# First attention with one combined VectorE operation and late division, two adaLN steps moved, and another order of ScalarE in the latent heads

## The reference

```python
# first block: attention that mixes three dilations (window, dilation):
DILATION_PATTERNS = ((128, 1), (512, 4), (2048, 16))   # 8 heads of 64
o = sum_d(wts_d * o_d) / sum_d(wts_d)   # wts_d = l_d * exp(m_d - max m)
# beside it: spatial gating u * (W_s LayerNorm(gelu(v)) + b), in chunks of 128
# adaLN: parameters of both later layers, from c and c_ctx only
m = silu(cond) @ w_ada + b_ada          # 1024 x 6144, for each of two layers
# latent attention of the last layer, 16 heads, 512 queries, 768 keys
s = einsum(q, k) * 96 ** -0.5; p = softmax(s); o = p @ v
```

## Time and profile before

| | us |
|---|---|
| median of 3 runs | 2501.7 (2501.55 to 2505.22) |
| profiled execution, and its span | 2504.9, 2503.1 |
| TensorE, VectorE, ScalarE busy | 2371.1, 1167.8, 752.2 |
| first attention | about 187 to 247 |
| experts of the first block | about 340 to 640 |
| latent heads | about 1797 to 2069 |

### The profile page before, as it was taken

The page is one execution under the profiler, slowest core; times in us unless marked ns, Lnnn a source line. Parts: engine busy times, 40 slices in busy tenths (PEclk is TensorE's granted clock), DMA queues, the critical chain, the costliest instruction groups (busy, mean ns, idle before and its releaser), DMA issues.

```text
span 2503.1 us, 29569 instructions
## 1 busy us (share of the span) xinstructions
PE 2371.1 (95%) x12236; PEld 1711.7 (68%) x12236; DVE 1167.8 (47%) x1912; ACT 752.2 (30%) x1303; POOL 224.8 (9%) x207
## 2 busy tenths in 40 slices
PE   8998999999898998899999999999888889999998
PEld 5673463333445978548888888877777767788886
DVE  2247342211564767543443343444676563544444
ACT  2235012111223345324112112123555562322222
POOL 0000011111104015100000000000202041000000
PEclk9999999999999999999999999999999999999999
DMA  9937659997410211312122112212010012223321
GB/s 350 372 130 269 247 178 391 376 379 293 164 23 31 68 51 52 135 34 82 53 68 68 61 41 84 68 34 61 30 51 5 18 68 74 86 86 101 98 86 69
DMA packets 172837, 308.80 MB, mean 123 GB/s; under 512 B 18459, under 2 KB 75155, under 8 KB 172576
## 3 DMA queue, kind: packets, MB, share of 16 engines
q1 hardware_dynamic: 159600, 278.40, 31.8%
q0 software_dynamic: 12368, 26.35, 3.0%
q10 hardware_dynamic: 736, 2.15, 0.2%
HBM read 355.05 MB, written 18.93 MB: 149 GB/s over the span
## 4 chain that ended last, share of the span: by engine, by line
PE 60%; DVE 8%; ACT 4%; issue 1%; DMA 0%; POOL 0%; DVEq 0%; ACTq 0%
PE PS L140 38%; PE PS L2593 11%; PE PS L2531 2%; PE PS L152 2%; PE PS L3180 2%; DVE X L110 1%; PE PS L2537 1%; DVE Rr L110 1%; PE PS L3101 1%; DVE H L110 1%; ACT X L130 1%; PE PS L2469 1%; DVE MIX L110 1%; DVE H L118 1%; DVE sm L121 1%
## 5 line engine op out<-in xcount | busy, mean ns | idle before, releaser
L140 PE MATMUL PS<-at,wH 128*128 128x512 f32 (+1 forms) x2144 | 564.6, 352 | 2.8 <-DVE at L110 2.8
L140 PEld LDWEIGHTS PS<-at,wH 128*128 128x128 f32 x2144 | 379.4, 190 | 57.7 <-DVE at L110 2.3
L140 PE MATMUL PS<-at,rest 128*128 128x512 f32 (+1 forms) x1072 | 377.0, 352 | 0.0
L2593 PE MATMUL PS<-wH,ac 128*128 128x512 f32 x880 | 277.8, 393 | 3.3 <-DVE hn L110 3.3
L110 DVE TENSOR_TENSOR rest<-ring,wH 128x2048 fp32r<-128x2048 f32 x66 | 150.4, 2291 | 212.6 <-ACT wH L133 212.0
L140 PEld LDWEIGHTS PS<-at,rest 128*128 128x128 f32 x1072 | 203.4, 190 | 27.1
L133 ACT CAST wH<-ring 128x2048 fp32r<-128x2048 f32 x66 | 124.6, 1906 | 264.5 <-PE PS L2593 199.8
L2593 PEld LDWEIGHTS PS<-wH,ac 128*128 128x128 f32 x880 | 165.2, 188 | 43.1 <-DVE hn L110 8.4
L2593 PE MATMUL PS<-rest,ac 128*128 128x512 f32 x440 | 171.4, 390 | 0.0
L140 PE MATMUL PS<-ring,AT 128*128 128x512 f32 x320 | 140.0, 593 | 1.4 <-ACT AT L133 0.8
L110 DVE TENSOR_TENSOR hn<-PS,gate 128x512 f32<-128x512 f32 x120 | 83.0, 692 | 104.4 <-PE PS L2593 99.4
(11 more groups left out here) (392 smaller groups left out, 4128.3 us busy)
## 6 DMA issues: line engine op xcount, KB each, us to landing
R<-in_w_gate_up_dram SPq DMA_DIRECT2D x32, 1024.0 KB
ring<-in_w_down_dram SPq DMA_DIRECT2D x32, 1024.0 KB, 14.1
ring<-in_w_gate_up_dram SPq DMA_DIRECT2D x32, 1024.0 KB
ring<-in_w_ffn_gate_dram SPq DMA_DIRECT2D x22, 1024.0 KB, 5.4
ring<-in_w_ffn_up_dram SPq DMA_DIRECT2D x22, 1024.0 KB, 5.4
ring<-in_w_ffn_down_dram SPq DMA_DIRECT2D x22, 1024.0 KB, 5.0
ring<-in_w_ada_dram SPq DMA_DIRECT2D x16, 1024.0 KB, 7.4
HIw<-in_w_gate_up_dram SPq DMA_DIRECT2D x16, 1024.0 KB
```

What stands on the lines that cost most here:

```text
L140: ins = self.e.matmul(out, l, r, start=k == 0, stop=k == len(pairs) - 1)
L2593: ins = p.e.matmul(bk(4 + n_dn % 3), a_, b_, start=start and i == 0, stop=stop and i == len(terms) - 1)
```

## The change

- The mask table is multiplied by 8. VectorE's two operations on a unit become one `tensor_tensor_reduce`: (score + 8 mask) x (-0.125), with the running minimum as second result; ScalarE's exponential takes scale -1 and that minimum as bias.
- The rows are no longer divided before they are turned; turns wait for the exponential alone. For each head pair VectorE takes 8 reciprocals at once, TensorE spreads them over 64 rows for both heads (eight products with the identity, into the bank whose turn it is, signal `linv`), VectorE copies them out, and multiplies them into o on its way from bank 5 to `mT`. ScalarE no longer copies o.
- adaLN steps 16 and 17 move from the attention into the projections: 16 behind the half product (9, 1), 17 in place of the wait for `ada_add` and of `keep_busy` before `spatial(3)`. The other six run at n = 6, 10, 14, 18, 22, 26.
- In the latent heads ScalarE exponentiates unit n before it copies the turned blocks of unit n - 2, where unit n - 2 is the first of its head.
- In the list of signal names the entries that these need are changed.

```diff
-    lnc = np.array([-1e30, 0.0, np.log(2.0), np.log(3.0)], np.float32)[c]
+    lnc = 8.0 * np.array([-1e30, 0.0, np.log(2.0), np.log(3.0)], np.float32)[c]
...
                 if n == 9 and t:
+                    if t == 1:
+                        ada_pe(p, 16)
                     spatial(t - 1)
 
         p.wait_ge(S("act1"), 15)
         scores1(p, 0)
-        p.wait_ge(S("ada_add"), 1)
-        keep_busy(p, 5, 9)
+        ada_pe(p, 17)
         spatial(3)
 
     def proj1_act(a):
@@ -804,7 +805,19 @@
...
-    ADA_AT = [n for n in range(35) if n % 8 in (4, 6)]
+    ADA_AT = [6, 10, 14, 18, 22, 26]
+    ml1 = lambda n: (sm[:, 2 * (n % 16):2 * (n % 16) + 1], sm[:, 2 * (n % 16) + 1:2 * (n % 16) + 2])
+    l8 = [sm[:, 16 * j:16 * j + 16].rearrange("p (n c) -> p n c", c=2)[:, :, 1] for j in range(2)]
+    inv8 = [sm[:, 32 + 8 * j:40 + 8 * j] for j in range(2)]
+    linv1 = AT[:, 4096:4608]
+    TURNS1 = [x for hp in range(4) for x in [("turn", 8 * hp + i) for i in range(8)] + [("inverse", hp)]]
+
+    def turned_bank(p, what):
+        i = TURNS1.index(what)
+        if i > 1:
+            kind, m = TURNS1[i - 2]
+            p.wait_ge(S("prob_T_copy" if kind == "turn" else "linv_copy"), m + 1)
+        return PTB[i % 2]
 
     def attn1_pe(p):
         p.wait_ge(S("act1"), 16)
@@ -812,7 +825,7 @@
         p.wait_ge(S("gated"), 4)
         p.wait_ge(S("v_copy"), 4)
         p.wait_ge(S("ada_add"), 1)
-        c = 16
+        c = 18
         for n in range(35):
 
             if n < 30 and n % 2 == 0:
@@ -830,56 +843,60 @@
             if 2 <= n < 34:
                 m = n - 2
                 nk, x = units1[m][1] + 1, xb[m % 4]
-                p.wait_ge(S("prob"), m + 1)
-                p.wait_ge(S("prob_T_copy"), m - 1)
-                p.turns([(bk(PTB[m % 2], 128, 128 * b), x[:, 128 * b:128 * b + 128]) for b in range(nk)], ident, S("prob_T"))
+                p.wait_ge(S("exp1"), m + 1)
+                b0 = turned_bank(p, ("turn", m))
+                p.turns([(bk(b0, 128, 128 * b), x[:, 128 * b:128 * b + 128]) for b in range(nk)], ident, S("prob_T"))
+                if m % 8 == 7:
+                    hp = m // 8
+                    p.wait_ge(S("inverse1"), hp + 1)
+                    b0 = turned_bank(p, ("inverse", hp))
+                    p.each([(PS[64 * e:64 * e + 64, 512 * b0 + 128 * t:512 * b0 + 128 * t + 128],
+                             inv8[hp % 2][:, 2 * t + e:2 * t + e + 1].to_broadcast([P, 64]), ident) for t in range(4) for e in range(2)], S("linv"))
             if n in ADA_AT:
                 ada_pe(p, c)
                 c += 1
 
     def attn1_dve(v):
-        c = 16
-        for n in range(35):
+        c = 18
+        for n in range(36):
             if n < 32:
                 h, t = units1[n]
                 w = 128 * t + 128
-                x, (m, l) = xb[n % 4], ml(n)
+                x, (m, l) = xb[n % 4], ml1(n)
                 v.wait_ge(S("score"), n + 1)
                 v.wait_ge(S("prob_T"), n - 3)
                 v.settle()
-                v.stt(x[:, 0:w], bk(SCORE[n % 4], w), 0.125, lnc[:, t, 0:w], ALU.mult, ALU.add, inc=S("masked"))
+                v.up(v.e.tensor_tensor_reduce(x[:, 0:w], bk(SCORE[n % 4], w), lnc[:, t, 0:w], -0.125, 3e38, ALU.add, ALU.min, m), S("masked"))
+            hp = n // 8 - 1
+            if hp >= 0 and n % 8 == 0:
+                v.wait_ge(S("exp1"), n)
+                v.recip(inv8[hp % 2], l8[hp % 2], inc=S("inverse1"))
+            if hp >= 0 and n % 8 == 2:
+                v.wait_ge(S("linv"), hp + 1)
+                v.copy(linv1, bk(PTB[TURNS1.index(("inverse", hp)) % 2]), inc=S("linv_copy"))
+            if hp >= 0 and n % 8 == 3:
+                v.wait_ge(S("o"), hp + 1)
                 v.settle()
-                v.red(m, x[:, 0:w], ALU.max, neg=True, inc=S("top"))
-            if 1 <= n <= 32:
-                w = 128 * units1[n - 1][1] + 128
-                x, (m, l) = xb[(n - 1) % 4][:, 0:w], ml(n - 1)
-                v.wait_ge(S("exp1"), n)
-                v.recip(l, l)
-                v.settle()
-                v.ts(x, x, l, None, ALU.mult, inc=S("prob"))
+                v.tt(mT[:, hp, :], bk(5), linv1, ALU.mult, inc=S("o_copy"))
             if n in ADA_AT:
                 ada_dve(v, c)
                 c += 1
 
     def attn1_act(a):
         a.wait_ge(S("gated"), 4)
-        c = 16
+        c = 18
         for n in range(35):
             if n < 32:
                 w = 128 * units1[n][1] + 128
-                x, (m, l) = xb[n % 4], ml(n)
-                a.wait_ge(S("top"), n + 1)
-                a.fn(x[:, 0:w], x[:, 0:w], ACT.Exp, inc=S("exp1"), bias=m, accum_out=l)
-            if n >= 3 and units1[n - 3][1] == 3 and units1[n - 3][0] % 2:
-                hp = units1[n - 3][0] // 2
-                a.wait_ge(S("o"), hp + 1)
-                a.cast(mT[:, hp, :], bk(5), inc=S("o_copy"))
+                x, (m, l) = xb[n % 4], ml1(n)
+                a.wait_ge(S("masked"), n + 1)
+                a.fn(x[:, 0:w], x[:, 0:w], ACT.Exp, inc=S("exp1"), bias=m, scale=-1.0, accum_out=l)
             if 2 <= n < 34:
                 m = n - 2
                 h, t = units1[m]
                 a.wait_ge(S("prob_T"), m + 1)
                 a.wait_ge(S("o"), h // 2)
-                a.cast(probT[h % 2][:, 0:t + 1, 128 * t:128 * t + 128], bk(PTB[m % 2], 128 * t + 128).rearrange("p (b q) -> p b q", b=t + 1),
+                a.cast(probT[h % 2][:, 0:t + 1, 128 * t:128 * t + 128], bk(PTB[TURNS1.index(("turn", m)) % 2], 128 * t + 128).rearrange("p (b q) -> p b q", b=t + 1),
                        inc=S("prob_T_copy"))
             if n in ADA_AT:
...
+        def turned(n):
+            t = units[n - 2][1]
+            a.wait_ge(S("p2_T"), 2 * (n - 2) + 1)
+            a.wait_ge(S("o2"), units[n - 2][0])
+            a.cast(pTm[:, 0:4, 128 * t:128 * t + 128], bk(4).rearrange("p (b q) -> p b q", b=4), inc=S("pT_act"))
+
         for n in range(67):
-            if 2 <= n < 66:
-                t = units[n - 2][1]
-                a.wait_ge(S("p2_T"), 2 * (n - 2) + 1)
-                a.wait_ge(S("o2"), units[n - 2][0])
-                a.cast(pTm[:, 0:4, 128 * t:128 * t + 128], bk(4).rearrange("p (b q) -> p b q", b=4), inc=S("pT_act"))
+            if 2 <= n < 66 and units[n - 2][1]:
+                turned(n)
             if n < 64:
                 x, (m, l) = pb[n % 3], ml(n)
                 b = 2 * (n % 2)
                 a.wait_ge(S("top2"), n + 1)
                 a.wait_ge(S("p2_T"), 2 * (n - 2))
                 a.fn(x, PS[:, 512 * b:512 * b + 768], ACT.Exp, inc=S("exp2"), bias=m, accum_out=l)
+            if 2 <= n < 66 and units[n - 2][1] == 0:
+                turned(n)
             if n >= 3 and units[n - 3][1] == 3:
                 h = units[n - 3][0]
```

More of the change, by code:

```diff
@@ L65 @@
     conv_w_T=("cond_T", 1), norm_w_T=("conv_w_T", 1), cq_a=("dt_raw", 2), kpe=("logit_m", 4), rows_T=("x_T", 8), proj6=("proj1", 40),
-    exp2=("exp1", 32), o2_copy=("o_copy", 4), pT_act=("prob_T_copy", 32),
+    exp2=("exp1", 32), pT_act=("prob_T_copy", 32),
     a_high=("x_high", 8), a_high0=("a_high", 8), a_high1=("a_high0", 6),
@@ L72 @@
     xb_copy=("h1_T_copy", 8), cq_copy=("z_copy", 12), cqb_copy=("cq_copy", 4), ck_copy=("g_silu", 12), kp_copy=("conv_silu", 8),
-    k_high=("conv_raw", 16), scaled=("cond", 1),
-    a_low=("x_low", 8), a_low0=("a_low", 8), a_low1=("a_low0", 6), q_low=("v_copy", 4), roped6=("roped1", 8), q_rope=("roped6", 8),
-    top2=("top", 32), prob2=("prob", 32), mixer_s=("mixer_r", 6), state_s=("state_r", 10),
+    k_high=("conv_raw", 16), scaled=("cond", 1), o2_copy=("scaled", 4),
+    a_low=("x_low", 8), a_low0=("a_low", 8), a_low1=("a_low0", 6), inverse1=("v_copy", 4), q_low=("inverse1", 4), linv_copy=("roped1", 8), roped6=("linv_copy", 4), q_rope=("roped6", 8),
+    mixer_s=("mixer_r", 6), state_s=("state_r", 10),
     gated_r=("gated", 4), y_sum_s=("gated_r", 6), z_gated=("y_sum_s", 6), v_mid=("combined", 4), gated_out0=("z_gated", 6),
@@ L78 @@
     ac_low0=("rowsD", 24), ac_low1=("ac_low0", 11), down_mul0=("y_copy0", 24), down_mul1=("down_mul0", 72),
-    down_add1=("down_add0", 72), ssd_norm=("vs_norm", 4), cq_norm=("ssd_norm", 6), ck_norm=("cq_norm", 4), k_low=("hid_T_copy", 24),
+    down_add1=("down_add0", 72), ssd_norm=("vs_norm", 4), cq_norm=("ssd_norm", 6), ck_norm=("cq_norm", 4), prob2=("ck_norm", 6), k_low=("hid_T_copy", 24),
     k_pe_low=("mixer_s", 6), cq_low=("inter_used_s", 10), ck_low=("state_s", 10), pe_low=("dt_mask", 6), wq_low=("q_decayed", 6),
```

2 lines of the change are left out of this document (1 added, 1 removed).

## The result

The changed kernel takes 2491.1 us (median of 5 runs, 2488.1 to 2491.8); beside it the kernel before took 2501.8 (2501.6 to 2505.2). The ratio is 0.9949, with a 95% interval of 0.9935 to 0.9962. The forecast was 2491.4. By the ratio the gain is 12.8 us (9.5 to 16.3) where the forecast had 10.3, so that the two medians lie 0.3 us apart is chance.

The account below looks back on a forecast made before the run. TensorE's list was taken to bound the attention, a ScalarE link the latent heads. Gains of 2.4 + 2.4 less 1.5 lost gave 3.3; with 7.0 from the heads, 10.3 off 2501.7: 2491.4 us, range 2484 to 2499.

Parts of the forecast that it names:

- the front: End of projections plus first attention: together 3.3 us earlier, bounds -2 and 8.5.
- Step 1, adaLN steps: End of projections: two adaLN steps move there and the fourth spatial product starts later; 1.5 us lost, bounds 0 and 3.3.
- Step 2, attention: First attention: VectorE's unit becomes one combined operation; 2.4 us won in the first head pair, 2.4 in the others together.
- TensorE's list: First attention: TensorE's own work, 12.2 us a head pair plus 1.0 of new products, limits what relieving VectorE can win.
- Second and third head pair: First attention: 13.2 us each against 13.59 and 13.48, so 0.4 and 0.3 us won.
- Fourth: First attention, last head pair: 11.0 us against 12.71, so 1.7 us won.
- First: First attention, first head pair: products with v at 202.0 instead of 204.4, 2.4 us won, bounds 0 and 4.5.
- Front in full: After the attention: an early gain is carried through in full, since an earlier route lets the experts' weight stream start earlier.
- rival (a): Projections and attention give nothing, TensorE being the bound already; only the heads win: 2494.7 or 2496.7 us, chance 0.16.
- Step 3, heads: Latent heads: ScalarE's exponential before its copy fits into idle time; 7.0 us won, bounds 3 and 9.
- ten links of the chain: Latent heads, where waits pass through ScalarE's copy and exponential: eight lose 0.90 us, two gain 0.47 and 0.59; 8.3 in all.
- Rival (c): Attention: the wait for a weight piece sets the low clock, which lasts through the fourth head pair; 2517 us, chance 0.06.

Follow-up runs that it names:

- experiment 5: The changed kernel again, unaltered: 2492.1 us, ratio 0.9952 to the kernel before.
- experiment 8: Changed kernel with the combined VectorE operation taken apart into mask-and-scale and a separate minimum, late division kept: 2493.8 us, ratio 0.9963 to the kernel before.
- experiment 4: Kernel before with only adaLN steps 16 and 17 moved to the end of the projections, old attention kept: 2513.9 us, ratio 1.0037.
- experiment 11: Changed kernel with the eight products that spread the reciprocals issued twice for each head pair: 2493.4 us, ratio 0.9956 to the kernel before.
- experiment 7: Changed kernel with only adaLN step 16 moved; step 17 stays in the attention, the old fillers and wait in its place: 2489.9 us, ratio 0.9943.
- experiment 2: Changed kernel with ScalarE's old order in the latent heads: 2498.3 us, ratio 0.9979 to the kernel before.
- experiment 1: Kernel before with only ScalarE's new order in the latent heads: 2494.3 us, ratio 0.9967.
- experiment 9: Kernel before with ScalarE's new order only at the ten heads where its chain of waits went over ScalarE's copy: 2494.4 us, ratio 0.9960.
- experiment 10: Kernel before with ScalarE's new order only at five other heads (1, 3, 6, 9, 11): 2503.4 us, ratio 0.9993.
- experiment 12: Changed kernel with only adaLN step 16 moved, and 28 instead of 22 fillers at the route: 2490.0 us, ratio 0.9945 to the kernel before.

## Why the prediction was right

The total was right, and so was its order: the heads first, the front second. The terms inside it were off by more than the total: the heads won more than the sum had, the adaLN steps were never seen to win, and the agreement to 0.3 us is luck.

**Step 1, adaLN steps: the mechanism right.** Step 16 in VectorE's shadow, the half product back at full speed (2.85 us, forecast 2.72), step 17 on a DMA wait at 182.38 (forecast 182.35), the fourth spatial product 1.76 us late (forecast 1.5). The clock's fall cost 1.4 us in step 17 and 0.2 in the spatial product, where 1.1 and 0.7 were forecast. In other traces the product was later, 2.8 us in experiment 5 and 3.5 in experiment 8; the stated bound of 3.3 is too low by the forecast's own terms, which give 2.1 + 1.1 + 0.7 = 3.9, and with it the front's lower bound of -2 should have been near -3. What was missing is that the same edit without the attention's costs 9 us (experiment 4). The two parts were priced one by one and summed, and in the traces they do not sum: 1.9 us for the attention and -9.6 for the steps in the front, 1.4 to 4.5 for both.

**Step 2, attention: the sum near, its parts not.** Forecast 4.8 us between the fourth spatial product and the output stage; measured 4.45 + 1.76 = 6.2 (4.2 in experiment 5). Right were the combined operation (0.69 us; its bound of 1.38 was not needed), VectorE's 5.7 us for a head pair (5.59), the spread products (1.0; 1.02) and TensorE's list as the main bound (experiment 11). Wrong was the 0.45 us for a VectorE copy of 512 columns from PSUM, which was also the lower bound of the operation: such a copy takes 0.69, in the trace before as well; VectorE had room for it. Of the operation the Trainium skill (Vector Engine (DVE) Microarchitecture Reference, 7. Points that are easy to get wrong) says half rate for two non-bf16 SBUF sources; with one source in PSUM the trace shows 691 ns, the mask-and-scale's own duration, so the rule did not apply here, and the read of the minimum, 83 ns, is the only extra.

- Second and third head pair: forecast 13.2 each, measured 13.48. TensorE's own list was 13.2 as said (13.17 busy in 13.50); what was left out is the 0.33 us in which it waits for ScalarE's copy of the turned blocks before the spread products; where the adaLN steps stand so that it does not wait, the pair takes 13.08 (experiment 7). Nothing was won in the third and 0.1 in the second, instead of 0.7 together.
- Fourth: forecast 11.0, measured 11.32.
- First: forecast 2.4 won, measured 2.90 + 1.76 = 4.7 from a later start. This is the attention's term that was most mis-sized, and it varies: 4.7 in this trace, 2.6 in that of experiment 5 (186.71 to 204.59 is 17.9 us, against 20.51). The clock was taken to rise at 197.3 as before; it was back at 193.0 in the first trace and at 198.1 in the second. The stated bound of 4.5 "by when the clock rises" is about what came.

**Front in full: supported by experiment 2,** whose time is 5.3 us less (3.0 to 7.3) and whose heads start 4.2 us earlier. The changed kernel's own two traces have the heads 0.6 earlier and 0.6 later than before, with falls of the clock on the way. Read alone, they would have supported rival (a).

**Step 3, heads: the mechanism right but not the whole of it.** Forecast 7.0 of 8.3 us, bounds 3 to 9; the stretch is 11.2 shorter in the trace, 8.3 (5 to 11) by experiment 1's ratio. The ten links of the chain held the places that pay (experiments 9 and 10). Over the steps that they touch the gains in the changed kernel are 0.8, 0.8, 2.6, 0.7, 2.4, 0.1, 0.1, 2.6, 0.2 and 0.6 us. The three large ones hold a fall of the clock before and none after: in the one shown, 0.9 is the exponential and 1.7 the products with v at 2.81 instead of 4.50. The clock has a share in the second 0.8 too: experiment 10, which does not edit that step, won 0.66 there. With 0.7 and three times 1.7 taken off, about 5.2 us are left for the links themselves, below the 7.0, since five links gave only 0.1 to 0.6: something else was next within less than 0.9, as the forecast allowed for. The missing term is the clock: nearly 6 us of the trace that the forecast did not have in its sum.

**Rival (c)** did not happen in the changed kernel, but experiment 4 is near that mechanism: a wait for a piece, a clock low through the first head pair, another fall in the last. It was argued against with "the same kinds of work present"; experiments 4 and 8 rather point to VectorE's shorter list, which leaves TensorE no stops in the changed kernel's last head pair beyond 0.56 us.

What stays open: why the clock of one and the same program falls at the experts or in the stages behind in one execution and not in another (changed kernel and experiment 2 at 340 to 350; experiments 5, 11 and 12 after 1000). That moves single traces by 3 to 4 us, as much as the whole front. Open is also whether the moved steps win anything: their gain in the front (2.6 us in one trace, none in the other) is within that spread.

## What to carry to other kernels

Where the chain of waits passes through an engine that has idled for the same releaser and then does two things, of which one was ready long ago, put the ready one first: ten such places gave 9.4 us in the trace, at five others the edit gave none. Price a stall of TensorE that goes or comes with what the clock does behind it: here that was about half of the heads' gain in the trace. Price two edits that feed the same engine together: moving two steps off the attention's list was worth -9 us with the old VectorE and was no loss with the new one. And before a trace's difference of 3 us, a hundred us away from any edit, is explained, take the same program again.

## What the runs showed of the hardware

- A VectorE multiply-add with a minimum beside it takes 691 ns for 128x512 from PSUM and SBUF in f32, as without the minimum, and is followed by a read of 83 ns; two of them stand 0.87 us apart (194.34 and 195.21).
- A VectorE copy of 512 f32 columns of 128 rows from PSUM took 692 ns here, no less than a product with a second operand (691).
- The clock fell at stops of TensorE of 2.9 to 3.2 us, in the stop or within 0.4 us of its end. It also fell at shorter ones: in one of 1.6 us (the kernel before, at 187.0), and at the end of the second of two stops of 1.4 and 1.5 us (experiment 4, at 246.3). The same stops do not always bring it down: in the last head pair of experiments 7 and 12 TensorE waits 0.97, 0.56 and 0.45 us alike, and the clock was low in the first from 239.4 to 242.8 and stayed up in the second.
- A wide f32 step of adaLN takes 3.64 us where the clock is low throughout and 1.92 at the full one, a factor of 1.9. The slow products with v of head 12, 4.50 us for 2.81, had the low clock for 3.4 us of their time, and lost half of that.
- Of one program, two traces had the clock at 0.87 and 0.70 in the same 13 us, and their profiled runs' times were alike within 1.5 us.
